# Another order of VectorE's work in the feed-forward pairs of a two-layer encoder

## The chip, the core and the metric

The kernel runs on one core of a Trainium2 chip. The metric is the device time of one execution in microseconds (us), the median of several runs. A profile of one execution gives the times of single instructions on the engines: TensorE (PE, with its weight loads apart as PEld), VectorE (DVE), ScalarE (ACT), GpSimd (POOL) and SyncE (SP), which issues DMAs.

## What is computed

A trunk of two layers is applied to two groups of token rows, 1024 and 256, of width 1024, in fp32. Each layer is a mixer (attention and spatial gating) and a feed-forward block, both normalised, modulated and gated by a condition. The change is in the feed-forward block:

```python
def _trunk(x, c, params):
    ...
    for l in range(DEPTH):
        ...
        x = x + ga1 * _rmsnorm(m, g_post_mix[l])
        h = _rmsnorm(x, g_pre_ffn[l]) * (1 + sc2) + sh2
        f = (jax.nn.silu(h @ w_gate[l]) * (h @ w_up[l])) @ w_down[l]
        x = x + ga2 * _rmsnorm(f, g_post_ffn[l])
```

The inner width of the block, D_FF, is 2816.

## The kernel before

**Products in three parts.** Every large matmul operand is held as a high half (rounded to fp32r) and a low half (what is left of it). `product` (L596 to L598) issues three matmuls for each product: low by high, high by low, high by high. Weights arrive by DMA in pieces of 128x1024 in three slots of `raw`; GpSimd makes the high half (L581, TENSOR_SCALAR) and the low half (L583, TENSOR_TENSOR) of each piece.

**The feed-forward block.** The 1280 token rows are worked in two halves of 640, and the 2816 inner columns in 22 tiles (`j`) of 128, two to a pair (`m`, 11 pairs). For each tile TensorE forms gate and up products with the inner columns on the partitions and the 640 tokens in two chunks (`c`) of 320, in the order gate chunk 0, gate chunk 1, up chunk 0, up chunk 1, in PSUM banks 0 to 3, 24 matmuls for each. These are the steps of one chunk afterwards:

- ScalarE: silu of the gate product, into `stage` (L1272)
- VectorE: `gated_product`, up product times silu, into `gated32` (L1669), "product 0" and "product 1" for the two chunks
- ScalarE: high half of that, into the ring in `ht_hi` (L1279)
- VectorE: `gated_low`, the low half, into the ring in `ht_lo` (L1675), "low 0" and "low 1"; both its inputs are in SBUF

A pair's down products follow one tile late: TensorE's order is gate and up of tile 2m, down products of pair m-1, gate and up of tile 2m+1. The down products of a pair are ten outputs (five token tiles by two column halves) of six matmuls of 512 columns each, which go in turn to PSUM banks 4 and 5. VectorE drains each into the accumulator in `tokm`: `add_down`, ten instructions, a copy (L1688) for the first pair of a half and an add (L1685) for the others. Output n may start when output n-2 has been drained (the semaphore `s_acc`). Before the down products of a pair TensorE waits for the low halves of both its tiles (`s_al`).

**What sets the order.** Each engine runs its instructions in the order in which the code lists them, and waits on semaphores. VectorE's order for a tile is in the loop over `m` and `j` at the end of its function: the products, the low halves, for an even tile (other than the first) the ten drains of the pair before, and then, in the second half of a layer, `residual` of a finished token tile of the first half (tiles 1 to 5). In layer 0 the normalising step of that token tile (`next_rows`, L1402) waits for a store and stands ahead of the next tile's products (`norm_waiting`). At some odd tiles the splitting of transposed rows for the next half or layer follows (L1358, L1359).

GpSimd takes a gate or up piece when the up products of two tiles before have ended, and a down piece when the down products before have, so its splits start at the end of an up product.

Of the kernel before, what the change touches and what calls it, by code (L numbers as in the profile page):

```python
# [33 lines left out]
def trunk_program(nc, a, y_prompt, y_sample):  # L34
# [41 lines left out]
    with ctx:  # L76
# [76 lines left out]
        def act_ring(half, s):  # L153
            return [h[:, s, (1 - half) * HTOK:(2 - half) * HTOK] for h in (ht_hi, ht_lo)]
# [120 lines left out]
        def ahead(l, half, j):  # L275

            if half == 0:
                return [("ffn", l, 1) + e for e in AHEAD.get(j, [])]
            return [("mix", l + 1, 0, NEXT_AHEAD[j])] if l + 1 < L and j in NEXT_AHEAD else []
# [175 lines left out]
        def pair_no(l, half, m): return (l * 2 + half) * PAIRS + m  # L455
        def tile_no(l, half, j): return (l * 2 + half) * FT + j
# [130 lines left out]
        def _(pe):  # L587
# [36 lines left out]
            for l in range(L):  # L624

                for e in z_order(l):
                    if e[0] == "tb":
                        _, gi, k = e
                        t0, nt = GROUPS[gi]
                        if k == 0:  # L630
                            pe.wait_ge(s_xn, xn_count(l, 0) + t0 + nt)
                        transposes(("mix", l, gi, k), [row_block(t0 + i, k) for i in range(nt)])
                    else:
                        _, c, t = e
                        n = Z[c][1] - Z[c][0]
                        if c == 0:
                            pe.wait_ge(s_ht, ht_count("mix", l, group_of(t)))
                        b = bank(("z", l, c, t))
                        w = w_block(c, KT, n)
                        for k in range(KT):  # L640
                            if t == 0:
                                pe.wait_ge(s_w, last_piece[(l, c, k)])
                            ins = product(ps[:, b, 0:n], act_cols(t, k), [x[:, k, :] for x in w], k == 0, k == KT - 1)
                        ins.then_inc(rdy[b], 1)
# [14 lines left out]
                for e in lora_order:  # L659
                    if e[0] == "tb":  # L660
                        _, gi, k = e
                        t0, nt = GROUPS[gi]
                        if k == 0:
                            pe.wait_ge(s_xn, xn_count(l, 1) + t0 + nt)
                        transposes(("lora", l, gi, k), [latent_block(t0 + i, k) for i in range(nt)])
                    else:
                        t = e[1]
                        pe.wait_ge(s_ht, ht_count("lora", l, group_of(t)))
                        for c in range(4):
                            b = bank(("qkv", l, t, c))  # L670
                            blk, kt, k0, n = (4, QKT, 0, H * QK) if c < 2 else (5, KVT, QKT, H * (NOPE + VD))
                            w = w_block(blk, kt, n)
                            o = c % 2 * n // 2
                            for k in range(kt):
                                if t == 0:
                                    pe.wait_ge(s_w, last_piece[(l, blk, k)])
                                ins = product(ps[:, b, 0:n // 2], act_cols(t, k0 + k), [x[:, k, o:o + n // 2] for x in w], k == 0, k == kt - 1)
                            ins.then_inc(rdy[b], 1)
# [628 lines left out]
        def _(dve):  # L1307
# [36 lines left out]
            def form_cols(l, which):  # L1344

                dve.wait_ge(s_cols, 16 * (15 * l + (10, 15)[which]))
                for g in range(2):
                    c = cols[:, g * KT:(g + 1) * KT]
                    ins = dve.scalar_tensor_tensor(c, c, 1.0, cols[:, PRE0:PRE0 + KT], ALU.add, ALU.mult)
                ins.then_inc(s_colr, 1)  # L1350
# [10 lines left out]
            def split_row_bank(key):  # L1361
                gi, k = key[-2:]
                split_bank(key, FFN_GROUPS[key[2]] if key[0] == "ffn" else GROUPS, gi, k)
# [8 lines left out]
            def residual(l, which, t):  # L1372

                r = res_no(l, which, t)
                c = tile_rstd(ST_TILE + 2 * (r % 2))
                if which and t:
                    form_gate(l, which, t)
                x = x_tile(t)
                link(dve.scalar_tensor_tensor(x, x, c, halves(gate_row[:, :]), ALU.mult, ALU.mult))  # L1379
                dve.wait_ge(s_xl, 16 * (r + 1))  # L1380
                dve.tensor_tensor(x, x, x_old[:, :, :], ALU.add).then_inc(s_res, 1)  # L1381

            def form_gate(l, which, t):

                if t in (0, TP):
                    n = (l * 2 + which) * 2 + (t > 0)
                    dve.wait_ge(s_gl, 32 * (n + 1))
                    dve.tensor_tensor(gate_row[:, :], gate_row[:, :], x_old[:, :, :].rearrange("p h c -> p (h c)"), ALU.mult).then_inc(s_gr, 1)
                    dve.wait_ge(s_gr, n + 1)
# [3 lines left out]
            def norm_waiting():  # L1393

                while waiting:
                    next_rows(*waiting.pop())
# [9 lines left out]
            for l in range(L):  # L1406
# [247 lines left out]
                for half in range(2):  # L1654
                    if half:
                        for gi in range(2):
                            for k in range(KT):
                                if k not in EARLY_K:
                                    split_row_bank(("ffn", l, 1, gi, k))
                        if l + 1 < L:  # L1660
                            form_cols(l + 1, 0)

                    def gated_product(j, c):
                        n = 2 * tile_no(l, half, j) + c
                        dve.wait_ge(s_u, n + 1)
                        dve.wait_ge(s_sil, n + 1)
                        if n >= 2:
                            dve.wait_ge(s_al, n - 1)
                        dve.tensor_tensor(gated32[:, c, :], ps[:, 2 + c, 0:320], stage[:, c * 320:(c + 1) * 320], ALU.mult).then_inc(s_a32, 1)  # L1669

                    def gated_low(j, c):
                        n = 2 * tile_no(l, half, j) + c
                        dve.wait_ge(s_ah, n + 1)
                        hi, lo = (x[:, c * 320:(c + 1) * 320] for x in act_ring(half, j % 4))
                        dve.tensor_tensor(lo, gated32[:, c, :], hi.bitcast(F32), ALU.subtract).then_inc(s_al, 1)  # L1675

                    def add_down(m):
                        for n in range(DPP):
                            t, c = divmod(n, 2)
                            k = DPP * pair_no(l, half, m) + n  # L1680
                            dve.wait_ge(s_dn, k + 1)
                            f = tokm[:, c, half * HT_ + t, :]
                            if m:
                                dve.wait_ge(s_acc, k - DPP + 1)
                                dve.tensor_tensor(f, ps[:, 4 + n % 2, :], f, ALU.add).then_inc(s_acc, 1)  # L1685
                            else:

                                dve.tensor_copy(f, ps[:, 4 + n % 2, :]).then_inc(s_acc, 1)  # L1688
                            if m == PAIRS - 1 and half == 1 and l == L - 1 and c and t:
                                residual(l, 1, HT_ + t - 1)  # L1690

                    for m in range(PAIRS):
                        for j in (2 * m, 2 * m + 1):
                            norm_waiting()
                            for c in range(2):
                                gated_product(j, c)
                            for c in range(2):
                                gated_low(j, c)
                            if j % 2 == 0 and m:
                                add_down(m - 1)  # L1700
                            if half == 1 and j == 0:
                                form_gate(l, 1, 0)
                            if half == 1 and 1 <= j <= HT_:
                                residual(l, 1, j - 1)
                                if l < L - 1:
                                    waiting.append((l, 1, j - 1))
                            for key in ahead(l, half, j):
                                split_row_bank(key)
                    add_down(PAIRS - 1)
# [36 lines left out]
```

## Time and profile before

| | |
|---|---|
| median of 3 runs | 3805.26 us (3804.15 to 3809.43) |
| span of the profiled execution | 3804.7 us |
| TensorE busy | 3386.0 us, 89% |
| VectorE busy | 1797.6 us, 47% |
| ScalarE busy | 1038.8 us, 27% |
| GpSimd busy | 1426.3 us, 37% |
| granted TensorE clock, mean | 0.953 |

The busy times are those of the whole span. The feed-forward halves lie, by the trace, at 969 to 1463, 1470 to 1985, 2788 to 3283 and 3289 to 3785 us. A granted clock of 1.00 is TensorE at its full 2.4 GHz, and 0.5 the lower level of 1.2 GHz. Matmuls overlap in the profile: a matmul of 512 columns is shown as 0.39 us long, while the next starts 0.23 us behind it.

### The profile page before, as it was taken

What the parts mean: (1) busy time and instruction counts of PE and PEld (TensorE: products, weight loads), DVE (VectorE), ACT (ScalarE), POOL (GpSimd) and SP (SyncE); (2) the same over time, 40 slices, a digit from 0 to 9 for tenths busy, and PEclk for the clock granted to TensorE, in tenths of its full rate; (3) what the DMA queues carried; (4) which work ended last, traced back from release to release, by engine and by line L of the source; (5) the groups of instructions that cost most, each with busy time, mean ns of one, the idle gap of its engine ahead of it and who ended that gap; (6) DMA issues with size and microseconds to landing.
All of it is one profiled execution on the core that took longest, in us unless ns stands there. A gap on an engine that the chain in (4) does not pass through costs nothing. (4 is left out here: it accounts for less than half of the span.)

```text
span 3804.7 us, 48831 instructions
## 1 busy us (share of the span) xinstructions
PE 3386.0 (89%) x19532; PEld 3033.0 (80%) x19532; DVE 1797.6 (47%) x2807; ACT 1038.8 (27%) x2298; POOL 1426.3 (37%) x804
## 2 busy tenths in 40 slices
PE   5998888888999998999988978888899999899997
PEld 2987677767888888888878777776788888888886
DVE  3116777754444534534433156786443453453333
ACT  2323555553100001200014234776320110120001
POOL 2210687810654544444530302000054454455441
PEclk7998899989999999999999988998999999999998
DMA  6205444422322223322222134112232222242222
GB/s 202 71 15 160 143 146 147 150 78 88 101 74 77 72 73 89 99 69 72 73 60 100 55 123 119 29 34 67 76 117 72 67 74 77 72 131 75 72 67 67
DMA packets 397728, 337.90 MB, mean 89 GB/s; under 512 B 107192, under 2 KB 325000, under 8 KB 397504
## 3 DMA queue, kind: packets, MB, share of 16 engines
q1 hardware_dynamic: 249808, 233.18, 20.1%
q10 hardware_dynamic: 147696, 101.61, 9.2%
q8 instruction: 156, 2.56, 0.3%
q14 instruction: 68, 0.56, 0.0%
HBM read 282.87 MB, written 51.87 MB: 88 GB/s over the span
## 5 line engine op out<-in xcount | busy, mean ns | idle before, releaser
L581 POOL TENSOR_SCALAR w_hi<-raw 128x1024 fp32r<-128x1024 f32 (+2 forms) x400 | 458.7, 1147 | 2270.2 <-PE ps L598 2135.0
L583 POOL TENSOR_TENSOR w_lo<-raw,w_hi 128x1024 fp32r<-128x1024 f32 (+2 forms) x400 | 975.4, 2438 | 33.4
L596 PE MATMUL ps<-w_lo,ht_hi 128*128 128x512 f32 (+2 forms) x2040 | 798.5, 391 | 145.8 <-DVE tokm L1685 83.3
L596 PE MATMUL ps<-ht_lo,w_hi 128*128 128x320 f32 x2816 | 873.3, 310 | 4.9 <-DVE ht_lo L1359 3.0
L597 PE MATMUL ps<-ht_hi,w_lo 128*128 128x320 f32 x2816 | 871.6, 310 | 0.0
L598 PE MATMUL ps<-ht_hi,w_hi 128*128 128x320 f32 x2816 | 871.5, 309 | 0.0
L597 PE MATMUL ps<-w_hi,ht_lo 128*128 128x512 f32 (+2 forms) x2040 | 787.1, 386 | 0.0
L598 PE MATMUL ps<-w_hi,ht_hi 128*128 128x512 f32 (+2 forms) x2040 | 784.9, 385 | 0.0
L596 PEld LDWEIGHTS ps<-w_lo,ht_hi 128*128 128x128 f32 x2040 | 397.8, 195 | 232.5 <-DVE tokm L1685 99.0
L596 PEld LDWEIGHTS ps<-ht_lo,w_hi 128*128 128x128 f32 x2816 | 530.0, 188 | 8.1 <-DVE ht_lo L1359 3.8
L597 PEld LDWEIGHTS ps<-ht_hi,w_lo 128*128 128x128 f32 x2816 | 530.0, 188 | 1.6
L598 PEld LDWEIGHTS ps<-ht_hi,w_hi 128*128 128x128 f32 x2816 | 530.0, 188 | 0.0
L1669 DVE TENSOR_TENSOR gated<-ps,stage 128x320 f32<-128x320 f32 x176 | 86.0, 491 | 806.1 <-PE ps L598 797.1
L598 PEld LDWEIGHTS ps<-w_hi,ht_hi 128*128 128x128 f32 x2040 | 397.8, 195 | 67.9
L597 PEld LDWEIGHTS ps<-w_hi,ht_lo 128*128 128x128 f32 x2040 | 398.4, 195 | 62.3
L1685 DVE TENSOR_TENSOR tokm<-ps,tokm 128x512 f32<-128x512 f32 x400 | 272.6, 689 | 253.9 <-PE ps L598 253.9
L1272 ACT ACTIVATE stage<-ps 128x320 f32<-128x320 f32 x176 | 75.8, 438 | 1011.6 <-PE ps L598 992.5
L1675 DVE TENSOR_TENSOR ht_lo<-gated,ht_hi 128x320 fp32r<-128x320 f32 x176 | 316.2, 1834 | 1.0
L1279 ACT ACTIVATE ht_hi<-gated 128x320 fp32r<-128x320 f32 x176 | 82.8, 472 | 549.3 <-DVE gated L1669 549.3
L607 PE MATMUL ps<-ident,tokm 128*128 128x128 f32 x580 | 106.6, 320 | 101.0 <-ACT tbank L936 47.8
L1548 DVE TENSOR_TENSOR ht_lo<-ps,ht_hi 128x512 fp32r<-128x512 f32 (+1 forms) x288 | 177.8, 653 | 35.7 <-ACT ht_hi L1149 34.7
L1537 DVE TENSOR_REDUCE stat<-ps 128x1 f32<-128x1024 f32 (+1 forms) x160 | 169.0, 1056 | 48.9 <-PE ps L598 48.2
(127 smaller groups left out, 3681.2 us busy)
## 6 DMA issues: line engine op xcount, KB each, us to landing
raw<-in_w_gate_dram SPq DMA_DIRECT2D x88, 512.0 KB, 3.8
raw<-in_w_up_dram SPq DMA_DIRECT2D x88, 512.0 KB, 3.8
raw<-in_w_down_dram SPq DMA_DIRECT2D x88, 512.0 KB, 3.5
raw<-in_w_mod_dram SPq DMA_DIRECT2D x80, 512.0 KB, 4.3
x_rows<-tokm ACTq DMA_DIRECT2D x30, 512.0 KB, 5.0
x_old<-x_rows ACTq DMA_DIRECT2D x30, 512.0 KB, 4.3
kv_rows<-stage ACTq DMA_DIRECT2D x20, 512.0 KB, 3.3
tokm<-kv_rows ACTq DMA_DIRECT2D x30, 320.0 KB, 4.1
```

Of the source, the lines that this page charges most:

```text
L581: pool.tensor_scalar(hi, r, 1.0, 0.0, ALU.mult, ALU.add).then_inc(s_whi, 1)
L583: pool.tensor_tensor(lo, r, hi.bitcast(F32), ALU.subtract).then_inc(s_w, 1)
L596: pe.matmul(out, lhs[0], rhs[1], start=first, stop=False)
L597: pe.matmul(out, lhs[1], rhs[0], start=False, stop=False)
L598: return pe.matmul(out, lhs[0], rhs[0], start=False, stop=last)
L607: ins = pe.transpose(ps[:, b, i * P:(i + 1) * P], src, ident[:, :])
L1279: act.activation(act_ring(half, j % 4)[0][:, c * 320:(c + 1) * 320], gated32[:, c, :], ACT.Copy).then_inc(s_ah, 1)
L1537: link(dve.tensor_reduce(c, psf[:, (u % 2) * 1024:(u % 2) * 1024 + w], AX.X, ALU.max))
L1548: dve.tensor_tensor(lo, ps[:, 4 + c, 0:w * P].rearrange("p (k q) -> p k q", q=P), hi.bitcast(F32), ALU.subtract).then_inc(s_ptl, 1)
L1669: dve.tensor_tensor(gated32[:, c, :], ps[:, 2 + c, 0:320], stage[:, c * 320:(c + 1) * 320], ALU.mult).then_inc(s_a32, 1)
L1675: dve.tensor_tensor(lo, gated32[:, c, :], hi.bitcast(F32), ALU.subtract).then_inc(s_al, 1)
L1685: dve.tensor_tensor(f, ps[:, 4 + n % 2, :], f, ALU.add).then_inc(s_acc, 1)
```

## The change

For each tile VectorE now does product 0, low 0, product 1, and low 1 last. For an even tile the ten drains of the pair before stand between product 1 and low 1. No instruction is added or taken away, and no other engine's code is touched.

```diff
                         for j in (2 * m, 2 * m + 1):
                             norm_waiting()
-                            for c in range(2):
-                                gated_product(j, c)
-                            for c in range(2):
-                                gated_low(j, c)
+                            gated_product(j, 0)
+                            gated_low(j, 0)
+                            gated_product(j, 1)
                             if j % 2 == 0 and m:
                                 add_down(m - 1)
+                            gated_low(j, 1)
                             if half == 1 and j == 0:
                                 form_gate(l, 1, 0)
```

The order on VectorE in the first half of layer 1, from the drains of pair 0 in tile 2 to those of pair 1 in tile 4, before; L1669 is the product, L1675 the low half:

```order
L1688 COPY tokm<-ps 128x512 x10
L1669 TENSOR_TENSOR gated32<-ps,stage 128x320 x2
L1675 TENSOR_TENSOR ht_lo<-gated32,ht_hi 128x320 x2
L1669 TENSOR_TENSOR gated32<-ps,stage 128x320 x2
L1675 TENSOR_TENSOR ht_lo<-gated32,ht_hi 128x320 x2
L1685 TENSOR_TENSOR tokm<-ps,tokm 128x512 x10
```

and of the changed kernel:

```order
L1688 COPY tokm<-ps 128x512 x10
L1675 TENSOR_TENSOR ht_lo<-gated32,ht_hi 128x320
L1669 TENSOR_TENSOR gated32<-ps,stage 128x320
L1675 TENSOR_TENSOR ht_lo<-gated32,ht_hi 128x320
L1669 TENSOR_TENSOR gated32<-ps,stage 128x320
L1675 TENSOR_TENSOR ht_lo<-gated32,ht_hi 128x320
L1669 TENSOR_TENSOR gated32<-ps,stage 128x320
L1675 TENSOR_TENSOR ht_lo<-gated32,ht_hi 128x320
L1669 TENSOR_TENSOR gated32<-ps,stage 128x320
L1685 TENSOR_TENSOR tokm<-ps,tokm 128x512 x10
L1675 TENSOR_TENSOR ht_lo<-gated32,ht_hi 128x320
```

Low 1 of an even tile has moved from ahead of the drains to behind them, and low 0 of every tile from behind product 1 to ahead of it.

VectorE in the second half of layer 0, from the normalising step ahead of tile 2 to the end of tile 2's work, before:

```order
L1402 TENSOR_SCALAR tokm<-tokm,stat 128x2x512
L1669 TENSOR_TENSOR gated32<-ps,stage 128x320 x2
L1675 TENSOR_TENSOR ht_lo<-gated32,ht_hi 128x320 x2
L1688 COPY tokm<-ps 128x512 x10
L1322 RECIPROCAL stat<-stat 128x1
L1379 SCALAR_TENSOR_TENSOR tokm<-tokm,stat,gate_row 128x2x512
L1381 TENSOR_TENSOR tokm<-tokm,x_old 128x2x512
```

and of the changed kernel:

```order
L1402 TENSOR_SCALAR tokm<-tokm,stat 128x2x512
L1669 TENSOR_TENSOR gated32<-ps,stage 128x320
L1675 TENSOR_TENSOR ht_lo<-gated32,ht_hi 128x320
L1669 TENSOR_TENSOR gated32<-ps,stage 128x320
L1688 COPY tokm<-ps 128x512 x10
L1675 TENSOR_TENSOR ht_lo<-gated32,ht_hi 128x320
L1322 RECIPROCAL stat<-stat 128x1
L1379 SCALAR_TENSOR_TENSOR tokm<-tokm,stat,gate_row 128x2x512
L1381 TENSOR_TENSOR tokm<-tokm,x_old 128x2x512
```

Low 1 now stands between the drains and the residual step (L1322, L1379, L1381) of a token tile.

## Rows read from the trace of the kernel before

**Rows 1.** The page's costliest groups: line, engine, operation, busy us, mean ns, idle before.

```profile
L1685 DVE TENSOR_TENSOR tokm<-ps,tokm 128x512 f32<-128x512 f32 x400 | 272.6, 689 | 253.9 <-PE ps L598 253.9
...
L1675 DVE TENSOR_TENSOR ht_lo<-gated,ht_hi 128x320 fp32r<-128x320 f32 x176 | 316.2, 1834 | 1.0
```

**Rows 2.** Waits of TensorE: waited for; us in total, times, longest us.

```profile
PE ps L596 <- DVE tokm L1685: 83.3, 37, 6.4
...
PE ps L596 <- DVE ht_lo L1675: 13.3, 4, 4.1
PE ps L596 <- DVE tokm L1688: 12.3, 4, 6.1
```

**Rows 3.** Time line of TensorE around one stall: start, us, instruction, [idle before].

```profile
2877.85 0.39 PE L598 MATMUL ps<-w_hi,ht_hi 128*128 128x512 f32 x1
...
2878.99 0.39 PE L597 MATMUL ps<-w_hi,ht_lo 128*128 128x512 f32 x1
2879.21 0.39 PE L598 MATMUL ps<-w_hi,ht_hi 128*128 128x512 f32 x1
2881.65 0.50 PE L596 MATMUL ps<-w_lo,ht_hi 128*128 128x512 f32 x1 [2.05 <-DVE tokm L1685]
2881.99 0.39 PE L597 MATMUL ps<-w_hi,ht_lo 128*128 128x512 f32 x1
```

**Rows 4.** Time line of VectorE around the same stall.

```profile
2873.38 0.49 DVE L1669 TENSOR_TENSOR gated<-ps,stage 128x320 f32<-128x320 f32 x1 [6.42 <-PE ps L598]
2876.90 0.49 DVE L1669 TENSOR_TENSOR gated<-ps,stage 128x320 f32<-128x320 f32 x1 [3.03 <-PE ps L598]
2877.30 3.69 DVE L1675 TENSOR_TENSOR ht_lo<-gated,ht_hi 128x320 fp32r<-128x320 f32 x2
2880.92 1.27 DVE L1685 TENSOR_TENSOR tokm<-ps,tokm 128x512 f32<-128x512 f32 x2
```

**Rows 5.** Time line of VectorE, 3010.5 to 3011.6: a later pair's low 0 alone.

```profile
3010.68 1.11 DVE L1675 TENSOR_TENSOR ht_lo<-gated,ht_hi 128x320 fp32r<-128x320 f32 x1
```

**Rows 6.** Time line of ScalarE in the stretch of rows 4.

```profile
2873.90 0.47 ACT L1279 ACTIVATE ht_hi<-gated 128x320 fp32r<-128x320 f32 x1 [3.61 <-DVE gated L1669]
```

**Rows 7.** Time line of GpSimd in the stretch of rows 4.

```profile
2871.47 2.42 POOL L583 TENSOR_TENSOR w_lo<-raw,w_hi 128x1024 fp32r<-128x1024 f32 x1
2877.02 1.06 POOL L581 TENSOR_SCALAR w_hi<-raw 128x1024 fp32r<-128x1024 f32 x1 [3.14 <-PE ps L598]
2878.16 2.49 POOL L583 TENSOR_TENSOR w_lo<-raw,w_hi 128x1024 fp32r<-128x1024 f32 x1
```

**Rows 8.** Time line of TensorE: its stalls at other down pairs.

```profile
1574.64 0.79 PE L596 MATMUL ps<-w_lo,ht_hi 128*128 128x512 f32 x1 [6.41 <-DVE tokm L1685]
...
1941.38 0.50 PE L596 MATMUL ps<-w_lo,ht_hi 128*128 128x512 f32 x1 [1.29 <-DVE tokm L1685]
...
2835.91 0.50 PE L596 MATMUL ps<-w_lo,ht_hi 128*128 128x512 f32 x1 [2.05 <-DVE tokm L1688]
...
2926.12 0.50 PE L596 MATMUL ps<-w_lo,ht_hi 128*128 128x512 f32 x1 [2.05 <-DVE tokm L1685]
...
3266.36 0.71 PE L596 MATMUL ps<-w_lo,ht_hi 128*128 128x512 f32 x1 [4.15 <-DVE ht_lo L1675]
```

**Rows 9.** Stretches: us, busy PE, PEld, DVE, ACT, POOL (instructions), clock, DMA share, GB/s.

```profile
2830.00:2840.00 10.00, 7.95 (x31) 6.25 (x30) 5.99 (x6) 0.47 (x1) 7.17 (x4) 0.83 0.29 92
2877.00:2887.00 10.00, 7.95 (x35) 6.23 (x34) 7.27 (x8) 0.47 (x1) 7.21 (x4) 1.00 0.32 91
```

**Rows 10.** Time line of VectorE in the second half of layer 0, before tile 4's drains.

```profile
1567.94 2.07 DVE L1402 TENSOR_SCALAR tokm<-tokm,stat 128x1024 f32<-128x1024 f32 x1 [4.38 <-DMA x_rows<-tokm]
1569.93 0.87 DVE L1669 TENSOR_TENSOR gated<-ps,stage 128x320 f32<-128x320 f32 x2
1570.95 3.04 DVE L1675 TENSOR_TENSOR ht_lo<-gated,ht_hi 128x320 fp32r<-128x320 f32 x2
```

**Rows 11.** Time line of GpSimd in the stretch of rows 10.

```profile
1571.00 2.64 POOL L583 TENSOR_TENSOR w_lo<-raw,w_hi 128x1024 fp32r<-128x1024 f32 x1
```

## The prediction

> **What bounds the kernel now.** I read the page's busy times first, then the waits, then the time line of each engine around one wait. TensorE is busy for 89% of the span, so the first question is where it isn't. The list of its waits names VectorE's adds of the down products (L1685, and L1688 for the first pair of a half) as the largest releaser: 83.3 us in 37 waits and 12.3 us in 4, that is 95.6 us in 41 waits [rows 2]. Of these 41, 35 are 2.04 or 2.05 us long, one is 1.29, three in the second half of layer 0 are 6.1 to 6.4, and two behind the very last adds make 4.0 together [rows 3, 8]. Four more waits, 13.3 us, are for the low half itself (L1675) at the start of the last down pair of a half [rows 2, 8].
>
> The reader should see in rows 3 and 4 how a 2.05 comes about. TensorE finishes the up product of chunk 1 at about 2876.9 and goes straight on to the down products, six matmuls for each of ten outputs, which alternate between two PSUM banks. The first two outputs need no one. The third needs the first bank drained, which is add 0. The first group's last matmul starts at 2877.85 and takes 0.39, so add 0 could start at about 2878.3. It starts at 2880.92 and TensorE goes on at 2881.65, 0.04 after its end. In between VectorE does product 1 (2876.90) and then both low halves, 3.69 us together [rows 4]. The same place one pair later splits these: the low half of chunk 0 took 1.11 [rows 5], so that of chunk 1 took about 2.6. GpSimd explains the size: it starts a weight split when the up product ends (2877.02), and the second low half ends just behind GpSimd's TENSOR_TENSOR (2878.16 + 2.49 = 2880.65) [rows 7]. The mean of L1675 is 1.83 us, for an operation that needs 0.5 to 0.6 where it is undisturbed [rows 1].
>
> **Part 1: the low half of chunk 0 goes ahead of product 1.** Product 0 runs at 2873.38 to 2873.87, ScalarE's high half at 2873.90 to 2874.37 [rows 4, 6]. VectorE then waits for the up product of chunk 1 until 2876.90. The low half fits there: it can start at 2874.4, 0.5 us after GpSimd has ended its last TENSOR_TENSOR (2871.47 + 2.42) [rows 7], and takes 0.5 to 0.6. The cover is 2.5 us wide. If GpSimd were still in an operation of 2.5, the low half would end at about 2877.4 and product 1 would be 0.5 us late, which add 0 still doesn't feel. Cost: nothing.
>
> **Part 2: the ten adds go ahead of the low half of chunk 1.** Product 1 ends at 2877.39, add 0 starts when its output is ready at 2878.3, ends at 2879.0, and TensorE needs the bank at 2879.44 (2879.21 and the usual step of 0.23). So the stall goes entirely, with 0.4 us to spare. The later adds (0.69 each) keep up with a group every 1.36 as they do now. What a stall costs is more than its idle time: from the last matmul before it to the second behind it, 2879.21 to 2881.99, is 2.78, where two usual steps make 0.46. That is **2.32 us** each [rows 3]. 35 x 2.32 = 81.2 us. The one of 1.29 gives 1.6 in the same way.
>
> Who waits for the low half of chunk 1, which now comes some 14 us later? The next down pair needs it, two tiles away (28 us). The next product on VectorE stands behind it, 10 us after the adds. ScalarE and the DMA queues issue nothing for it. It costs nothing in 36 of the pairs.
>
> **Part 3: the clock.** TensorE's granted clock is 1.00 through most of these stretches, but behind 5 of the 36 stalls of up to 2.05 us it falls to the lower level for a few microseconds: the window 2830 to 2840 shows 0.83, where 2877 to 2887, with the same stall, shows 1.00 [rows 9]. The pair behind the first is 45.74 us long (2835.91 to 2881.65), the next 44.47 [rows 3, 8], so such a fall costs 1.3. The five, worked out so, cost 1.3, 1.6, 1.7, 1.3 and 1.6, together 7.3 (one has its rows). With no idle time there I expect them gone. Bounds: 0 and 7.3. I take 7.3, since no pair without a stall in it shows a fall.
>
> **Part 4: the last pair of each half.** There the down products need the low half of chunk 1 at once, and TensorE waits 4.15 us (the row at 3266.36, and one like it at 1446.90), 3.40, and, by subtraction from the 13.3, 1.6 [rows 2, 8]. Now VectorE does product 1, low 0, low 1. Afterwards it does product 1 (0.49), waits for ScalarE's high half (0.47), and does low 1 alone. GpSimd begins its TENSOR_SCALAR 0.12 behind the start of product 1 and its TENSOR_TENSOR 1.14 later [rows 4, 7]. Low 1 would be issued some 1.04 behind the start of product 1, 0.2 ahead of that TENSOR_TENSOR, which is the place where low 0 gets through today, ending 0.25 behind the TENSOR_TENSOR's start (issued 2877.30, 1.11 long) [rows 4, 5, 7]. Then it saves 2.5 us. If it misses, it waits 2.5 us as today and nothing is saved. I take 2.5, 2.5, 1.0 and 0: 6.0, bounds 0 and 7. The clock that falls behind such waits may give back 2 more (0 to 4).
>
> The Trainium skill, "SBUF — State Buffer", section "SBUF: two separate sides", says that VectorE with two SBUF inputs and GpSimd take a shared port pair for a whole instruction, and that the loser blocks fully. The trace's 1.11 and 2.6 agree with that. By this rule the saving here is all or nothing, and it does not tell who is served when both wait; losing each race would make the sum 6 us smaller.
>
> **Part 5: the first three pairs of the second half of layer 0.** Here VectorE is late for another reason: it finishes a token tile, waits for the store of it (4.38 us on the DMA) and normalises it (2.07) before product 0, which starts at 1569.93 though TensorE has long ended the up products [rows 10]. In the new order VectorE must wait for ScalarE between product 0 and low 0 (0.5 us, covered today), and low 0 is issued at about 1571.08, within 0.1 us of GpSimd's TENSOR_TENSOR at 1571.00 [rows 11]. If it wins, add 0 starts at about 1571.9, 2.0 earlier than today's 1573.9. If it loses, low 0 ends at about 1573.9 and add 0 starts 0.5 later than today. Besides, the low half that now follows the adds delays the next token tile by some 0.8 us. For the first of the three (product 0 at about 1518.9) GpSimd's order favours VectorE and I put it at 2.2 saved. Together 3.5, bounds 6 saved and 4 lost.
>
> **The sum** against the profiled execution, whose span is 3804.7: 81.2 + 1.6 + 7.3 + 6.0 + 2.0 + 3.5 = 101.6, so a span of 3703.1. The median of the runs (3805.26) is 0.6 above the profiled span. Forecast: **3703.7 us**, 2.7% less. Differences below 0.2% (8 us) couldn't be told from no change.
>
> **The rivals.**
>
> A, the port races are lost, at the half ends and in the three late pairs. For it: the races are within 0.1 to 0.2 us. Against: low 0 gets through in the same place today. The 6.0 goes and the 3.5 becomes about a loss of 1: 3714 us, chance 0.12.
>
> B, the clock still falls as often, because what makes it fall is not the short stalls. For it: 31 stalls of the same length have no fall. Without the 9.3 of parts 3 and 4: 3713 us, chance 0.08.
>
> C, a new wait takes half of the gain. The place would be the hand-over itself, add 0 and TensorE's third group, where 0.4 us of slack is left. If each of the 35 pairs kept 1.1 us, the time would be 3742. Against it: from the third group on, today's trace has the same hand-over at the same pace without idle time. Chance 0.03.
>
> D, slower. Low 0 now stands ahead of product 1 and so of add 0. If GpSimd, which works through up to three weight pieces of 3.5 us in a row at an odd tile's end, were to shut VectorE out for two pieces instead of one operation, low 0, issued at 2874.4, would get through at 2881.4 and end at 2881.9, and add 0 would start behind product 1 at 2882.4, 1.5 later than now. 40 pairs x 1.5 = 60 us: 3865. It decides as soon as low 0 ends after about 2880.5. Against it: two low halves together take 3.69 with GpSimd at work [rows 4], and GpSimd is idle from 2873.9 to 2877.0 [rows 7]. Chance 0.02.
>
> E, no change: the order of the instructions is what the change says on VectorE, so this needs another releaser to end at the same time as add 0. The page shows none; chance 0.01.
>
> The forecast has 0.74. The range takes in the bounds: best 3696 (7 and 4 in part 4, 6 in part 5), worst about 3726 (nothing in parts 3 and 4, 4 lost in part 5); it holds A and B too. Faster 0.97, same 0.01, slower 0.02.
>
> **What would show it.** In the trace after: L1685 and L1688 no longer among the large releasers of TensorE, 36 waits gone; a pair at 42.1 us instead of 44.5; the mean of L1675 down to 0.6 to 1.1; product 1 of an even tile followed by an idle 0.9 us and add 0; granted clock 1.00 right through the first half of each layer. Wrong would be: an idle TensorE ahead of the third group of a pair, a product 1 that starts behind the end of the up product, or stalls over 7 us in the second half of layer 0.

## The result, and the profile after

| | before | after |
|---|---|---|
| median of the runs | 3807.35 us (4 runs) | 3696.78 us (4 runs, 3693.36 to 3702.42) |
| ratio of after to before | | 0.9713 (95%: 0.9691 to 0.9736) |
| span of the profiled execution | 3804.7 us | 3700.6 us |
| TensorE busy | 3386.0 us, 89% | 3361.9 us, 91% |
| VectorE busy | 1797.6 us | 1606.2 us |
| GpSimd busy | 1426.3 us | 1405.7 us |

The changed kernel is 2.9% faster. The median of before has moved by 2 us against the table further up, since one more run is in it. The same instructions keep VectorE busy for 191 us less. One group, the low halves, takes 207 us less; the others change by up to 28 us either way and add 15 together. The two groups that answer to [rows 1], the first from the page of after, the second from the list of its groups by shape:

```profile
L1685 DVE TENSOR_TENSOR tokm<-ps,tokm 128x512 f32<-128x512 f32 x400 | 276.2, 692 | 276.8 <-PE ps L598 276.8
```

```profile
L1675 DVE TENSOR_TENSOR ht_lo<-gated,ht_hi 128x320 fp32r<-128x320 f32 x176 | 109.4, 621 | 73.2 <-ACT ht_hi L1279 73.2
```

The low half takes 0.62 us in the mean, where it took 1.83; the adds take what they took. The waits of TensorE after, to be held against [rows 2]:

```profile
PE ps L596 <- DVE tokm L1685: 12.3, 4, 4.2
...
PE ps L596 <- DVE ht_lo L1675: 6.4, 4, 1.6
...
PE ps L596 <- DVE tokm L1688: 4.0, 1, 4.0
```

Of 41 waits for a drain 5 are left: three in the second half of layer 0 and the two behind the last adds. All 36 of 2.05 us or less are gone. The time line of VectorE around the place that answers to [rows 4], one pair in the first half of layer 1 (start, us, instruction, idle before):

```profile
2816.03 0.49 DVE L1669 TENSOR_TENSOR gated<-ps,stage 128x320 f32<-128x320 f32 x1 [9.04 <-PE ps L598]
2817.06 0.49 DVE L1675 TENSOR_TENSOR ht_lo<-gated,ht_hi 128x320 fp32r<-128x320 f32 x1 [0.54 <-ACT ht_hi L1279]
2819.55 0.49 DVE L1669 TENSOR_TENSOR gated<-ps,stage 128x320 f32<-128x320 f32 x1 [2.00 <-PE ps L598]
2820.93 0.69 DVE L1685 TENSOR_TENSOR tokm<-ps,tokm 128x512 f32<-128x512 f32 x1 [0.89 <-PE ps L598]
...
2833.78 0.91 DVE L1675 TENSOR_TENSOR ht_lo<-gated,ht_hi 128x320 fp32r<-128x320 f32 x1
```

and of TensorE where [rows 3] had the stall:

```profile
2821.64 0.39 PE L597 MATMUL ps<-w_hi,ht_lo 128*128 128x512 f32 x1
2821.87 0.39 PE L598 MATMUL ps<-w_hi,ht_hi 128*128 128x512 f32 x1
2822.09 0.39 PE L596 MATMUL ps<-w_lo,ht_hi 128*128 128x512 f32 x1
2822.32 0.39 PE L597 MATMUL ps<-w_hi,ht_lo 128*128 128x512 f32 x1
```

Low 0 lies in the wait for the up product, VectorE waits 0.89 for TensorE instead of the other way round, and the third group (2822.09) follows the second in the usual step of 0.22. From one even tile's product 1 to the next (below, the period) it is 42.11 or 42.21 us in most pairs, where it was 44.45 to 44.49 or 44.55 to 44.59, and 41.78 where no transposes lie in it, instead of 44.12 to 44.17.

### The profile page after: what moved, and what is told of

Read it like the earlier page. It is cut to its first block and busy times, and to the rows that moved or that the text cites. A ratio compares the mean times of both kernels' runs of the same rounds, so it can differ in the third digit from the quotient of the medians.

```text
span 3700.6 us, 48831 instructions
## 1 busy us (share of the span) xinstructions
PE 3361.9 (91%) x19532; PEld 3027.5 (82%) x19532; DVE 1606.2 (43%) x2807; ACT 1039.0 (28%) x2298; POOL 1405.7 (38%) x804
## 5 line engine op out<-in xcount | busy, mean ns | idle before, releaser
L581 POOL TENSOR_SCALAR w_hi<-raw 128x1024 fp32r<-128x1024 f32 (+2 forms) x400 | 438.6, 1097 | 2185.9 <-PE ps L598 2044.3
L596 PE MATMUL ps<-w_lo,ht_hi 128*128 128x512 f32 (+2 forms) x2040 | 786.1, 385 | 57.5 <-DVE ht_lo L1359 22.2
L1669 DVE TENSOR_TENSOR gated<-ps,stage 128x320 f32<-128x320 f32 x176 | 86.5, 491 | 783.1 <-PE ps L598 774.1
L1685 DVE TENSOR_TENSOR tokm<-ps,tokm 128x512 f32<-128x512 f32 x400 | 276.2, 692 | 276.8 <-PE ps L598 276.8
L607 PEld LDWEIGHTS ps<-ident,tokm 128*128 128x128 f32 x580 | 79.6, 163 | 128.6 <-ACT tbank L936 37.9
```

The costliest lines, as they stand in the source:

```text
L581: pool.tensor_scalar(hi, r, 1.0, 0.0, ALU.mult, ALU.add).then_inc(s_whi, 1)
L596: pe.matmul(out, lhs[0], rhs[1], start=first, stop=False)
L607: ins = pe.transpose(ps[:, b, i * P:(i + 1) * P], src, ident[:, :])
```

## The experiments

Each kernel was timed beside the kernel before (3809.6 in the first four experiments, 3809.1 in the last four), and a ratio is to that. The intervals of the changed kernel (0.9691 to 0.9736) and of the first three experiments overlap almost wholly, so their medians alone don't rank them. Where a few microseconds matter I also compare, in the profiled executions, the time from VectorE's first feed-forward product to the end. It leaves out the part ahead of it, which is the same code in all kernels and differs by up to 10 us between the executions. I split it in three. "Halves" is the sum of the four feed-forward halves, each from product 1 of its first tile to product 1 of its last. "Mixer" lies between the end of layer 0's last half and product 1 of layer 1's first tile. "Rest" is mainly the ends of the other three halves, with the last down pair of each.

| us | halves | mixer of layer 1 | rest | together |
|---|---|---|---|---|
| before | 1853.2 | 836.4 | 134.3 | 2823.9 |
| changed | 1752.5 | 830.7 | 128.5 | 2711.6 |
| low 0 alone | 1758.0 | 832.1 | 128.9 | 2718.9 |
| drains alone | 1745.1 | 837.3 | 136.3 | 2718.7 |
| even tiles alone | 1750.6 | 832.3 | 135.5 | 2718.4 |
| GpSimd held | 1737.4 | 838.7 | 126.7 | 2702.8 |
| low 1 second | 1783.5 | 831.8 | 125.6 | 2740.9 |
| norm late | 1734.5 | 828.7 | 127.8 | 2691.0 |
| norm late, split wait | 1734.5 | 827.2 | 120.7 | 2682.3 |
| all together | 1735.0 | 827.1 | 120.8 | 2682.9 |

The mixer's code is the same in all of them and it takes 827 to 839 us; the wait at the end of the half ahead of it, of 0 to 3.4 us, explains only a part. So a few microseconds of the last column mean little unless they stand in the halves or the rest.

**Low 0 ahead of product 1, nothing else.**

```diff
-                            for c in range(2):
-                                gated_product(j, c)
-                            for c in range(2):
-                                gated_low(j, c)
+                            gated_product(j, 0)
+                            gated_low(j, 0)
+                            gated_product(j, 1)
+                            gated_low(j, 1)
                             if j % 2 == 0 and m:
                                 add_down(m - 1)
```

> One part of the change alone: low 0 goes ahead of product 1, the ten drains stay behind low 1 (product 0, low 0, product 1, low 1, drains). Theory P (what kept add 0 back was the wait for GpSimd's TENSOR_TENSOR of 2.4 to 2.5 us, and one low half issued before it gets through): low 1 is issued about 1.04 us behind the start of product 1, gets through at GpSimd's TENSOR_SCALAR's end, and add 0 starts about 1.5 us behind product 1's start. The 36 stalls of 2.05 and less are gone, pair period 42.1 us, time 3697 +- 8 as with the full change. Rival Q (the drains' move carries the gain): low 1 waits the TENSOR_TENSOR out, pair period stays at 44.5 us, time about 3795 to 3805.

Measured: 3702.6 us, ratio 0.9719 (0.9705 to 0.9734). VectorE and GpSimd at an even tile:

```profile
2823.71 0.49 DVE L1669 TENSOR_TENSOR gated<-ps,stage 128x320 f32<-128x320 f32 x1 [2.00 <-PE ps L598]
2824.74 0.49 DVE L1675 TENSOR_TENSOR ht_lo<-gated,ht_hi 128x320 fp32r<-128x320 f32 x1 [0.54 <-ACT ht_hi L1279]
2825.16 0.68 DVE L1685 TENSOR_TENSOR tokm<-ps,tokm 128x512 f32<-128x512 f32 x1
```

```profile
2823.84 1.06 POOL L581 TENSOR_SCALAR w_hi<-raw 128x1024 fp32r<-128x1024 f32 x1 [3.37 <-PE ps L598]
2824.98 2.51 POOL L583 TENSOR_TENSOR w_lo<-raw,w_hi 128x1024 fp32r<-128x1024 f32 x1
```

Theory P holds and Q falls. The drains still stand behind low 1, but low 1 is issued 0.24 us ahead of GpSimd's TENSOR_TENSOR, takes 0.49 and ends 0.33 behind GpSimd's TENSOR_SCALAR. Add 0 starts 1.45 behind product 1, where it took 4.02 [rows 4], and the period is 42.11. Ordinary pairs need no more than this half of the change. The three late pairs of layer 0 do: the halves take 5.5 us more than with the full change, and the difference lies there.

**The drains ahead of both low halves, nothing else.**

```diff
                             for c in range(2):
                                 gated_product(j, c)
+                            if j % 2 == 0 and m:
+                                add_down(m - 1)
                             for c in range(2):
                                 gated_low(j, c)
-                            if j % 2 == 0 and m:
-                                add_down(m - 1)
```

> The other part alone: the ten drains go ahead of both low halves, which stay behind product 1 (product 0, product 1, drains, low 0, low 1). Both theories: add 0 no longer stands behind a low half, pair period 42.1 us. The last pair of a half has low 0 and low 1 behind product 1 as in the kernel before, so TensorE waits 4.15, 4.15, 3.40 and 1.61 there, some 7 us in all more than with the full change, and the clock falls there again (+2 to +5). In the second half of layer 0 add 0 starts 1.1 us earlier than with the full change, while the token tile behind it starts 0.5 to 2.5 later. Time 3703 to 3712.

Measured: 3704.9 us, ratio 0.9716 (0.9700 to 0.9733), and 2718.7 from the first product to the end, 7.1 more than the full change: 7.4 less in the halves, 7.8 more in the rest and 6.6 more in the mixer. The period is 42.11 again, so either part alone removes the ordinary stalls. The waits of TensorE show what each part does elsewhere:

```profile
PE ps L596 <- DVE ht_lo L1675: 13.3, 4, 4.1
...
PE ps L596 <- DVE tokm L1685: 10.2, 4, 3.2
...
PE ps L596 <- DVE tokm L1688: 2.9, 1, 2.9
```

The half ends are back at their 13.3 us of before. The three late pairs of layer 0 are 2.92, 3.22 and 2.93 here, 3.96, 4.25 and 3.96 with the full change, and 6.12, 6.39 and 6.12 with low 0 moved alone. So it is the drains' move that shortens those, and low 0 ahead of them costs 1.0 of it: the 0.5 for ScalarE's high half, and its own 0.5. In time it costs more than that idle time. From product 1 of tile 2 to that of tile 8 (before, the full change, this run, and low 0 alone; columns as in [rows 9], with the clock third from the end):

```profile
1519.30:1667.70 148.40, 131.60 (x745) 121.98 (x746) 71.88 (x76) 32.10 (x57) 66.08 (x34) 0.93 0.30 93
```

```profile
1500.20:1638.80 138.60, 129.28 (x745) 120.25 (x746) 59.00 (x75) 31.85 (x56) 63.14 (x33) 0.95 0.32 98
```

```profile
1502.50:1635.00 132.50, 125.21 (x746) 117.31 (x747) 68.48 (x76) 32.17 (x57) 64.05 (x34) 0.99 0.34 104
```

```profile
1497.40:1642.80 145.40, 129.56 (x746) 120.52 (x747) 61.53 (x76) 31.92 (x56) 64.96 (x33) 0.93 0.30 94
```

The granted clock is 0.99 here against 0.95, and the stretch is 6.1 us shorter than with the full change. In this execution the drains' move alone is the better order for the late pairs, and low 0's move is the better one for the ends of the halves.

**The new order on even tiles alone.**

```diff
-                            for c in range(2):
-                                gated_product(j, c)
-                            for c in range(2):
-                                gated_low(j, c)
-                            if j % 2 == 0 and m:
-                                add_down(m - 1)
+                            if j % 2 == 0:
+                                gated_product(j, 0)
+                                gated_low(j, 0)
+                                gated_product(j, 1)
+                                if m:
+                                    add_down(m - 1)
+                                gated_low(j, 1)
+                            else:
+                                for c in range(2):
+                                    gated_product(j, c)
+                                for c in range(2):
+                                    gated_low(j, c)
```

> The full new order on even tiles alone, the old one on odd tiles. The last tile of a half is odd, so its waits go back to 4.15, 4.15, 3.40 and 1.61 us (6.4 in the changed kernel); the other pairs keep a period of 42.1 us. If the saving at the half ends is the odd tiles' part, the time is 3697 + 7 and 2 to 5 for the clock: 3704 to 3709. The rival, that the odd tiles' order also carries something in the other pairs, would show in a period over 42.1 us.

Measured: 3703.5 us, just under the 3704 to 3709 expected, ratio 0.9720 (0.9704 to 0.9736); from the first product to the end 2718.4, 6.8 more than the full change. TensorE at the end of layer 0's second half and of layer 1's first:

```profile
1915.38 0.50 PE L596 MATMUL ps<-w_lo,ht_hi 128*128 128x512 f32 x1 [3.40 <-DVE ht_lo L1675]
...
3181.52 0.50 PE L596 MATMUL ps<-w_lo,ht_hi 128*128 128x512 f32 x1 [4.15 <-DVE ht_lo L1675]
```

The waits at the half ends are those of before to the hundredth, and the ordinary pairs have the periods of the full change. The rest takes 7.0 us more, the halves 1.9 less. So the odd tiles' order is worth the half ends, 6.9 us of idle time, and nothing that shows in the other pairs.

**VectorE as before, GpSimd held back.** For gate and up pieces, all but those of a layer's first two tiles, GpSimd waits for the low halves; for down pieces and those of the mixer it waits as before.

```diff
-                        pool.wait_ge(s_u, 2 * (tile_no(l, 0, b) - 1))
+                        pool.wait_ge(s_al, 2 * (tile_no(l, 0, b) - 1))
```

> VectorE's order is that of the kernel before; GpSimd alone is changed: for the gate and up pieces it waits for the two low halves of the tile (semaphore of L1675) instead of the up products, so it starts some 1.5 us later and no longer works while VectorE makes low halves. Theory P (port): L1675 takes 0.5 us each time, add 0 starts 1.5 us behind product 1's start, the 36 stalls are gone without any move on VectorE, period 42.1 us, half ends 1.6 us each, time about 3697 to 3702. Rival R (two low halves ahead of the drains are too much in themselves, whoever else works): stalls stay at over 1 us each, time over 3750.

Measured: 3686.4 us, some 11 below the low end of what I expected, ratio 0.9680 (0.9664 to 0.9697), and 2702.8 us from the first product to the end, 8.8 less than the change under study (15.1 less in the halves, 8.0 more in the mixer), with not one instruction of VectorE moved. VectorE and GpSimd at an even tile of layer 1:

```profile
2802.97 0.49 DVE L1669 TENSOR_TENSOR gated<-ps,stage 128x320 f32<-128x320 f32 x1 [3.03 <-PE ps L598]
2803.37 1.12 DVE L1675 TENSOR_TENSOR ht_lo<-gated,ht_hi 128x320 fp32r<-128x320 f32 x2
2804.40 0.68 DVE L1685 TENSOR_TENSOR tokm<-ps,tokm 128x512 f32<-128x512 f32 x1
```

```profile
2804.65 1.06 POOL L581 TENSOR_SCALAR w_hi<-raw 128x1024 fp32r<-128x1024 f32 x1 [3.50 <-DVE ht_lo L1675]
```

Both low halves take 1.12 us together instead of 3.69 [rows 4], and add 0 is in time. Rival R falls: it was never the number of instructions ahead of add 0. Two waits of layer 0's second half stay as before, against the expectation, the stall of 1.29 and the last pair's 3.39. There GpSimd already splits pieces of the next mixer, which the edit doesn't hold back, and the two low halves still take 0.9 and 2.1. What I had not foreseen is the late pairs of layer 0, which all but close (0.37, 0.54, 0.35). Ahead of the one that answers to [rows 10]:

```profile
1527.57 0.76 DVE L1402 TENSOR_SCALAR tokm<-tokm,stat 128x1024 f32<-128x1024 f32 x1 [3.15 <-DMA x_rows<-tokm]
1528.23 0.88 DVE L1669 TENSOR_TENSOR gated<-ps,stage 128x320 f32<-128x320 f32 x2
1529.26 0.90 DVE L1675 TENSOR_TENSOR ht_lo<-gated,ht_hi 128x320 fp32r<-128x320 f32 x2
```

The normalising step takes 0.76, not 2.07, and the low halves 0.90, not 3.04. Those pairs, too, were late by GpSimd's work.

**Low 1 between drain 0 and drain 1.** A move to where it should do harm, if the place in GpSimd's sequence is what counts. `add_down` calls it ahead of its second output.

```diff
                             gated_product(j, 1)
                             if j % 2 == 0 and m:
-                                add_down(m - 1)
-                            gated_low(j, 1)
+                                add_down(m - 1, lambda: gated_low(j, 1))
+                            else:
+                                gated_low(j, 1)
...
-                    def add_down(m):
+                    def add_down(m, behind_first=None):
                         for n in range(DPP):
+                            if n == 1 and behind_first:
+                                behind_first()
```

> The changed kernel with one move: on even tiles low 1 stands between drain 0 and drain 1. It is then issued about 2.1 us behind the start of product 1, in the middle of GpSimd's first TENSOR_TENSOR (1.26 to 3.7 behind it). Theory P (the place in GpSimd's sequence decides, not the number of instructions ahead of a drain): low 1 takes about 2 us instead of 0.5, drain 1 ends some 4.7 us behind product 1's start where TensorE's fourth group wants its bank at 3.9; an idle 0.7 us ahead of the fourth group and a period of 42.9 to 43.1, 36 times 0.9 = 32 us, time 3725 to 3735. Rival R (the order alone): low 1 takes 0.5, drain 1 is in time, period 42.1, time 3697.

Measured: 3730.6 us, ratio 0.9797 (0.9781 to 0.9813), and a period of 43.01. VectorE, GpSimd and TensorE there (the edit adds two lines, so L1687 is the add, L1685 elsewhere):

```profile
2829.47 0.69 DVE L1687 TENSOR_TENSOR tokm<-ps,tokm 128x512 f32<-128x512 f32 x1 [0.89 <-PE ps L598]
2830.07 2.03 DVE L1675 TENSOR_TENSOR ht_lo<-gated,ht_hi 128x320 fp32r<-128x320 f32 x1
2832.03 1.27 DVE L1687 TENSOR_TENSOR tokm<-ps,tokm 128x512 f32<-128x512 f32 x2
```

```profile
2829.35 2.41 POOL L583 TENSOR_TENSOR w_lo<-raw,w_hi 128x1024 fp32r<-128x1024 f32 x1
```

```profile
2832.76 0.50 PE L596 MATMUL ps<-w_lo,ht_hi 128*128 128x512 f32 x1 [0.61 <-DVE tokm L1687]
```

The same low half, issued 0.7 us into GpSimd's TENSOR_TENSOR, takes 2.03 and ends 0.34 behind it. An idle time of 0.61 costs 0.90 a pair (43.01 less 42.11), which also agrees with the extra 0.27 (2.32 less 2.05) that the prediction put on each stall. Issued 1.03 behind the start of product 1, as in the first run, low 1 takes 0.49; issued 1.99 behind it, here, it takes 1.5 more.

**The normalising step behind the tile's work.** In the changed kernel:

```diff
-                            norm_waiting()
                             gated_product(j, 0)
                             gated_low(j, 0)
                             gated_product(j, 1)
                             if j % 2 == 0 and m:
                                 add_down(m - 1)
                             gated_low(j, 1)
+                            norm_waiting()
```

> The changed kernel with the normalising step (L1402) of a finished token tile behind the tile's products, drains and low halves instead of ahead of them. It matters in the second half of layer 0 alone, where three down pairs keep stalls of 3.96, 4.25 and 3.96. If these stalls are the wait for the store plus the step itself ahead of product 0, they go, with 0.3 each for the restart and 5 to 7 for the clock that falls behind them: time 3697 - 12 - 1 - 6 = 3678, periods there near 42.2. If instead the products are late because GpSimd stretches the residual steps, part stays: over 3685.

Measured: 3679.7 us, ratio 0.9661 (0.9646 to 0.9675). From the first product to the end 2691.0, 20.7 less than the changed kernel. TensorE's waits for drains:

```profile
PE ps L596 <- DVE tokm L1685: 4.2, 3, 2.5
```

The three late stalls are gone but for 0.15; the rest are the two at the very end.

**And TensorE's wait at the half ends split.** On top of that kernel:

```diff
-                        pe.wait_ge(s_al, 2 * tile_no(l, half, 2 * m + 2))
+                        pe.wait_ge(s_al, 2 * tile_no(l, half, 2 * m + 2) - 1)
...
                             t, c = divmod(n, 2)
+                            if n == 4:
+                                pe.wait_ge(s_al, 2 * tile_no(l, half, 2 * m + 2))
```

> As the run with the late normalising step, and at the last pair of a half TensorE starts the down products of token tiles 0 and 1 once low 0 is there, and waits for low 1 only ahead of token tile 2. The four waits of 1.61 go, 1.9 each with the restart: 7.5 us less than that run, about 3670. If the wait only moves to the drains (add 0 or the fifth output), less.

Measured: 3667.8 us, ratio 0.9630 (0.9616 to 0.9644). L1675 is no longer among what TensorE waits for. From the first product to the end 2682.3, 8.7 less than the run before it, where 7.5 were expected; 7.1 of it are in the rest and 1.5 in the mixer. It has the lowest median of the study.

**All together**: TensorE's split wait as above, the order product 0, low 0, product 1, low 1, drains, normalising step on VectorE, and GpSimd held, for the first block of layer 1 too (GpSimd's part of the edit):

```diff
-                        pool.wait_ge(s_u, 2 * (tile_no(l, 0, 0) - first))
+                        pool.wait_ge(s_al, 2 * (tile_no(l, 0, 0) - first))
...
-                        pool.wait_ge(s_u, 2 * (tile_no(l, 0, b) - 1))
+                        pool.wait_ge(s_al, 2 * (tile_no(l, 0, b) - 1))
```

> All that helped in one kernel: GpSimd held until the low halves are there (also for the first block of layer 1), VectorE in the order product 0, low 0, product 1, low 1, drains, normalising step, and TensorE's split wait at the last pair. Against the run with the late normalising step and the split wait it should save nothing on the stalls, which are gone there too, if both remove the same wait: 3668 to 3672. If GpSimd's hold also frees VectorE elsewhere, below that; if the weights come late, above.

Measured: 3672.1 us, ratio 0.9641 (0.9627 to 0.9656); from the first product to the end 2682.9 against 2682.3. The intervals of the two overlap. Holding GpSimd adds nothing that can be measured once VectorE's order avoids it: both remove the same wait.

## Why the prediction was right

The forecast was 3703.7 us in a range of 3696 to 3726; 3696.8 is at its fast end. The 3696 is not what its own bounds give: 1.0 and 2.0 more in part 4 and 2.5 more in part 5 take 5.5 us off 3703.7, which is 3698.2. So the measured median lies 1.4 us beyond what the terms allow, and that it fell inside the stated range is luck. By its steps:

**The bound and part 1** held. Low 0 takes 0.49 in the wait for the up product, product 1 starts when the up product is ready.

**Part 2** held in mechanism and size: 2.34 to 2.39 us a stall by the periods, against 2.32. But the prediction gave the gain to the drains' move alone. The first run shows that low 0's move does it as well, by letting low 1 through ahead of GpSimd; in the sum that makes no difference, for someone who wants to choose one of the two it does.

**Part 3**, the clock, held. In the pairs of the kernel before, the outliers were 45.7 to 46.2, five of them; after, no pair outside the late three is over 42.3. (Its five costs as written add to 7.5; the 7.3 comes from the unrounded periods.) The clock still falls behind longer stalls, here in two stretches of after, at the first late pair and at the second (columns as in [rows 9]):

```profile
1498.00:1508.00 10.00, 6.68 (x18) 5.30 (x19) 4.71 (x8) 3.56 (x6) 4.39 (x3) 0.66 0.36 107
1549.00:1559.00 10.00, 8.86 (x32) 7.13 (x33) 4.55 (x9) 3.09 (x5) 2.32 (x1) 0.83 0.32 93
```

**Part 4** held: low 1 wins the race at all half ends. TensorE's waits are 1.61 each, so 2.54, 2.54, 1.79 and 0 were saved, 6.9 against 6.0. On the clock behind these waits the prediction put 2.0. Behind the 3.40 the granted clock was 0.66 (1969 to 1979, before), behind the 1.61 in the same place 1.00 (1919.5 to 1929.5, after), so something was given back there; how much isn't settled, since the mixer follows at once.

**Part 5** had the mechanism half right and was sized too small, 3.5. Low 0 won the race there in each of the three pairs. VectorE and GpSimd at the second of them:

```profile
1545.33 2.33 DVE L1402 TENSOR_SCALAR tokm<-tokm,stat 128x1024 f32<-128x1024 f32 x1 [4.35 <-DMA x_rows<-tokm]
1547.58 0.48 DVE L1669 TENSOR_TENSOR gated<-ps,stage 128x320 f32<-128x320 f32 x1
1548.59 0.49 DVE L1675 TENSOR_TENSOR ht_lo<-gated,ht_hi 128x320 fp32r<-128x320 f32 x1 [0.54 <-ACT ht_hi L1279]
```

```profile
1548.65 2.68 POOL L583 TENSOR_TENSOR w_lo<-raw,w_hi 128x1024 fp32r<-128x1024 f32 x1
```

It is 0.06 us ahead. The stalls shrank by 2.15, 2.16 and 2.15, 6.5 in all, and the stretch from tile 0 to tile 8 by 8.7, at a granted clock that was 0.95 and not 0.93 from tile 2 on. The race was no open one. In the kernel before the low half of chunk 0 already took 0.49 in each of these three pairs, issued 0.05 ahead of GpSimd's TENSOR_TENSOR, and low 0 was now issued at the same distance behind product 0 (1.01, against 1.02), not the 0.13 later that the prediction worked out. I had read the cause of the lateness as the wait for the store and the step of 2.07 itself; the run with GpSimd held showed that most of that step's length was GpSimd's too. Moving the step away (20.7 us) and keeping GpSimd out of its way are two cures for the same delay.

**The sum.** The pairs gave 100.8 us in the four halves, where parts 2, 3 and 5 had 93.6. The rest of the time behind the first feed-forward product gave 11.6, where part 4 had 8.0; of it 5.8 are in the rest and 5.7 in the mixer of layer 1, where only 1.8 us of idle time were saved and the remainder can't be told from the mixer's own differences between executions. Against these 112.3 us the span fell by 104.1 only, because the part ahead of the first feed-forward matmul, the same instructions in both kernels, took 8.3 us longer in this execution. Before and after:

```profile
969.19 0.39 PE L596 MATMUL ps<-ht_lo,w_hi 128*128 128x320 f32 x1 [0.99 <-ACT tokm L1249]
```

```profile
977.49 0.39 PE L596 MATMUL ps<-ht_lo,w_hi 128*128 128x320 f32 x1 [0.99 <-ACT tokm L1249]
```

The profiled execution is the slowest of the four of after (3702.4); the median is 5.6 below it. So the profiled span's closeness to the forecast (3700.6 against 3703.1) owes something to chance: the gain was some 9 to 11 us larger than my sum, by the medians (110.6) and by the 112.3.

**The rivals.** A: the races were not lost, in either place. B: the clock did not keep falling. C: no half of the gain was kept; add 0 has 0.4 us of slack, and the run with low 1 behind drain 0 shows what using up such slack costs. D: low 0 is never shut out in an ordinary pair, it takes 0.49; only in the first tile of each layer, with no drains behind it, it waits for GpSimd and takes 1.68. E: the stalls went, and TensorE waits for nothing else in their place.

**Open.** The races that bear on the gain were won in all profiled executions; how often other timing would lose them wasn't tried. It can happen: in the run with the split wait one low 0 at an odd tile was issued 0.01 us behind the start of a TENSOR_TENSOR and took 2.7. Nor was it settled which stalls make the clock fall. It fell behind 5 of 36 of up to 2.05 us before, behind none of the four of 1.61 after, and behind one of the three late ones with the drains' move alone (the one of 3.22, not the two of 2.9). Each count is from one execution of its kernel.

## What to carry to other kernels

When an instruction takes 1.1 us in one place and 2.6 in another for the same shape, look at what the other engine is doing at its start before counting it as work: here the cure was to issue it 0.2 us ahead of GpSimd's long operation, or to hold GpSimd back by one semaphore, and neither removed an instruction. Drains on which TensorE waits should stand ahead of work that nobody wants soon, and a stall costs its idle time and 0.3 us for the restart. Two cures of the same wait don't add: look at the waits after the first one.

## What the runs showed of the hardware that I had not expected

A VectorE operation with both inputs in SBUF (the low half) that is issued while GpSimd's TENSOR_TENSOR of 2.4 us runs ends 0.34 to 0.35 us behind it, whatever is left of it (2.03 long when issued 0.7 into it, 2.6 when issued just behind its start). Behind GpSimd's TENSOR_SCALAR of 1.06 it ends 0.33 later in the same way. An add that reads PSUM and `tokm` takes its 0.69 beside the same TENSOR_TENSOR (2829.47 in the run with low 1 second). The normalising TENSOR_SCALAR, with one tensor input in SBUF, suffers too: 2.07 and 2.33 us, each ending 0.55 behind a TENSOR_TENSOR of GpSimd's, and 0.76 with GpSimd idle. Between the two lies nothing: in the ten traces each of the 284 low halves issued 0.01 to 0.25 us ahead of the start of a TENSOR_TENSOR of GpSimd's took 0.48 to 0.50, and each of the 222 issued 0.01 to 0.21 us behind such a start took 2.1 to 2.7.
